# Weight halves behind the root, squares ahead of copies, and a root spread from four row groups to four banks

## The reference

```python
def rmsnorm(x, g):
    xf = x.astype(jnp.float32)
    y = xf * lax.rsqrt(jnp.mean(xf * xf, axis=-1, keepdims=True) + NORM_EPS)
    return (y * g.astype(jnp.float32)).astype(x.dtype)

    # in hybrid_layer
    x = x + rmsnorm(mixed @ w_out, norm_mix_post)
    h = rmsnorm(x, norm_ffn_pre)
    ...
    x = x + rmsnorm((jax.nn.gelu(ua) * ub) @ w_down, norm_ffn_post)
    x = x + rmsnorm(gate * e, norm_ple)
```

## Time and profile before

| | us |
|---|---|
| median of 3 runs | 4541.85 |
| lowest, highest | 4536.22, 4552.05 |
| profiled execution, first to last instruction | 4542.0 |
| TensorE busy in it | 4202.5 (93%) |
| VectorE busy | 1966.0 (43%) |
| ScalarE busy | 1514.9 (33%) |

### The profile page before, as it was taken

How to read it: one execution, slowest core, us unless ns; L and a number is a source line. 1 busy time by engine, 2 the same in 40 slices (tenths; PEclk the granted TensorE clock), 3 DMA queues, 4 the chain that set the end, 5 groups by cost and what they waited for, 6 DMA issues and landing times.

```text
span 4542.0 us, 73530 instructions
## 1 busy us (share of the span) xinstructions
PE 4202.5 (93%) x32028; PEld 3257.7 (72%) x32028; DVE 1966.0 (43%) x2957; ACT 1514.9 (33%) x2699; POOL 570.2 (13%) x402
## 2 busy tenths in 40 slices
PE   8899779899998999779899998988899999999999
PEld 6676776677776676776677776755688888667877
DVE  4536434455335536434455334357332231443332
ACT  3533233333333533233333333247221121343221
POOL 1215100011002215100011001012000000150000
PEclk9999899899998999999899998999999999999999
DMA  4122002244322132003244321100111111101222
GB/s 159 38 102 70 31 4 93 70 173 172 142 84 104 38 107 70 31 4 107 79 172 167 136 85 41 52 28 1 38 53 64 65 61 61 56 6 61 93 90 92
DMA packets 97681, 351.69 MB, mean 77 GB/s; under 512 B 10064, under 2 KB 13648, under 8 KB 95952
## 3 DMA queue, kind: packets, MB, share of 16 engines
q1 hardware_dynamic: 86480, 313.02, 20.0%
q10 hardware_dynamic: 10880, 33.96, 2.0%
HBM read 332.26 MB, written 14.68 MB: 76 GB/s over the span
## 4 chain that ended last, share of the span: by engine, by line
PE 82%; DVE 7%; ACT 3%; issue 3%; POOL 3%; ACTq 0%; DMA 0%; DVEq 0%; POOLq 0%; SPq 0%
PE ps L350 20%; PE ps L351 19%; PE ps L353 19%; PE ps L1344 7%; PE ps L2370 1%; PE ps L1889 1%; PE ps L391 1%; DVE sml L2445 1%; POOL e L2901 1%; ACT whi L297 1%; PE ps L2814 1%; POOL dd L1194 1%; PE ps L864 1%; POOL ops L1210 1%; POOL ops L1202 1%
## 5 line engine op out<-in xcount | busy, mean ns | idle before, releaser
L307 DVE TENSOR_TENSOR wlo<-ring,whi 128x1024 fp32r<-128x1024 f32 x494 | 623.7, 1263 | 1876.0 <-ACT whi L297 1875.6
L297 ACT CAST whi<-ring 128x1024 fp32r<-128x1024 f32 x494 | 517.4, 1048 | 2139.3 <-PE ps L353 1875.3
L350 PE MATMUL ps<-h_hi,whi 128*128 128x512 f32 x1424 | 597.1, 419 | 16.3 <-DVE h_lo L443 8.9
L351 PE MATMUL ps<-h_lo,whi 128*128 128x512 f32 x1424 | 569.2, 400 | 0.0
L353 PE MATMUL ps<-h_hi,wlo 128*128 128x512 f32 x1424 | 567.9, 399 | 0.0
L350 PE MATMUL ps<-hm_hi,whi 128*128 128x512 f32 (+1 forms) x1408 | 514.4, 365 | 16.5 <-DVE hm_lo L446 15.1
L351 PE MATMUL ps<-hm_lo,whi 128*128 128x512 f32 (+1 forms) x1408 | 480.3, 356 | 0.0
L353 PE MATMUL ps<-hm_hi,wlo 128*128 128x512 f32 (+1 forms) x1408 | 418.5, 355 | 0.0
L350 PEld LDWEIGHTS ps<-h_hi,whi 128*128 128x128 f32 x1424 | 272.9, 192 | 158.7 <-issue 62.4
L350 PE MATMUL ps<-ac_hi,whi 128*128 128x512 f32 x880 | 329.7, 375 | 3.0 <-DVE wlo L307 3.0
L350 PEld LDWEIGHTS ps<-hm_hi,whi 128*128 128x128 f32 x1408 | 267.1, 190 | 86.9 <-DVE hm_lo L446 20.4
(11 more groups left out here) (385 smaller groups left out, 7255.6 us busy)
## 6 DMA issues: line engine op xcount, KB each, us to landing
ring<-in_w SPq DMA_DIRECT2D x590, 512.0 KB, 3.3
h_spill<-h ACTq DMA_DIRECT2D x2, 2048.0 KB, 6.7
x_spill<-x ACTq DMA_DIRECT2D x2, 2048.0 KB, 14.6
m_spill<-m ACTq DMA_DIRECT2D x2, 2048.0 KB, 10.0
h_again<-h_spill ACTq DMA_DIRECT2D x2, 2048.0 KB, 8.9
ma<-m_spill ACTq DMA_DIRECT2D x2, 2048.0 KB, 10.1
x<-x_spill ACTq DMA_DIRECT2D x2, 2048.0 KB, 9.9
x<-in_x SPq DMA_DIRECT2D x4, 512.0 KB, 7.8
```

Of the source, the lines that this page charges most:

```text
L297: self.A.copy(self.hi[k % 2][:], raw).then_inc(self.s_cut_hi.h, 1)
L307: self.V.tensor_tensor(self.lo[k % 2][:], raw, self.hi[k % 2][:].bitcast(F32), ALU.subtract).then_inc(self.s_cut_lo.h, 1)
L350: T.matmul(ps[:, b, 0:cw], hi, xh(q, c0, cw), start=q == 0, stop=False, skip_group_check=True)
L351: T.matmul(ps[:, b, 0:cw], hi, xl(q, c0, cw), start=False, stop=False, skip_group_check=True)
```

## The change

Three edits to the norms.

1. **Cuts behind the root.** The dense products that end in a norm get `hold` = the last column's piece + 1, so that the piece after that is no longer cut ahead of the last column's work. `add_normed` and `norm_to` take `cut`: ScalarE makes that cut right behind `stat_root`, VectorE right behind `stat_inverse` and ahead of its wait for the spread. It is used at 9 norms: Z, ZF and E in both hybrid layers, and the three `mod_norm`s behind an `add_gated`. `first_cuts` of the first norm becomes `cut=1`, which is the same.
2. **Square, then copy.** For Z and ZF each column is squared from PSUM first and copied after.
3. **Four row groups to four banks.** Where four banks are given, `stat_spread` issues one matmul per quarter of the tokens whose operands are 32 partitions high (rows 32g to 32g+31 of the picking matrix and of `inv`), each into its own bank, and VectorE reads the spread as 4 pieces of 128 from four banks (`spread_of`, with the tile viewed alike by `by_bank`). It is used at 8 norms: the hybrid layers' first norms, Z, the norm behind Z, and E, in both layers. ZF keeps one bank and the `mod_norm`s two, with the old spread.

The lines added and taken away (unchanged lines left out):

```diff
@@ -396,6 +396,14 @@
+        if len(banks) == 4:
+            for g in range(4):
+                one = CONST["ident"] + 32 * g
+                rows = slice(32 * g, 32 * g + 32)
+                m = T.matmul(self.ps[:, banks[g], 0:w], self.con[rows, one:one + 1].to_broadcast([32, P]),
+                             self.inv[rows, 0:w], start=True, stop=True, skip_group_check=True)
+            m.then_inc(self.s_rsq.h, 1)
+            return
@@ -405,8 +413,18 @@
+    def spread_of(self, banks, si, cw):
+        if len(banks) == 4:
+            return self.ps[:, banks[0]:banks[0] + 4, 0:P]
+        return self.ps[:, banks[si], 0:cw]
+    def by_bank(self, banks, t):
+        return t.rearrange("p (g c) -> p g c", c=P) if len(banks) == 4 else t
-                first_cuts=False):
+                cut=None):
@@ -425,8 +443,8 @@
-            if first_cuts:
-                self.act_cuts(1)
+            if cut is not None:
+                self.act_cuts(cut)
@@ -449,13 +467,14 @@
-            if first_cuts:
-                self.dve_cuts(1)
+            if cut is not None:
+                self.dve_cuts(cut)
-                    i = V.scalar_tensor_tensor(dst[:, j, c0:c0 + cw], self.X[:, j, c0:c0 + cw], gain(j, si),
-                                               ps[:, banks[si], 0:cw], ALU.mult, ALU.mult)
+                    i = V.scalar_tensor_tensor(self.by_bank(banks, dst[:, j, c0:c0 + cw]),
+                                               self.by_bank(banks, self.X[:, j, c0:c0 + cw]), gain(j, si),
+                                               self.spread_of(banks, si, cw), ALU.mult, ALU.mult)
@@ -464,10 +483,10 @@
-    def add_normed(self, Z, gain, st, sums, pe_first=None, pe_last=None, act_last=None, dve_pair=None):
-        V, G, ps = self.V, self.G, self.ps
+    def add_normed(self, Z, gain, st, sums, banks, pe_first=None, pe_last=None, act_last=None, dve_pair=None, cut=None):
+        V, G = self.V, self.G
@@ -475,23 +494,28 @@
-            self.stat_spread(st, [st.bank])
+            self.stat_spread(st, banks)
+            if cut is not None:
+                self.act_cuts(cut)
+            if cut is not None:
+                self.dve_cuts(cut)
-                    V.scalar_tensor_tensor(Z[:, i, :], Z[:, i, :], gain(i), ps[:, st.bank, :], ALU.mult,
+                    z = self.by_bank(banks, Z[:, i, :])
+                    V.scalar_tensor_tensor(z, z, gain(i), self.spread_of(banks, 0, S), ALU.mult,
@@ -638,8 +662,8 @@
-        b_lo = self.norm_to(h, SEG1, lambda j, si: self.p1(gain, j), [6], st, h_hi, h_lo, ready=ready,
-                            first_cuts=layer == 0)
+        b_lo = self.norm_to(h, SEG1, lambda j, si: self.p1(gain, j), (4, 5, 6, 7), st, h_hi, h_lo, ready=ready,
+                            cut=1 if layer == 0 else None)
@@ -1851,24 +1875,24 @@
+            self.stat_square(st, n, ps[:, 2 + n % 4, :])
-            self.stat_square(st, n, ps[:, 2 + n % 4, :])
-                       pe_tick=pe_z, act_tick=act_z))
-        return self.first_norms(Z, b_z, st)
-    def first_norms(self, Z, b_z, st):
+                       pe_tick=pe_z, act_tick=act_z, hold=cols_z[-1][-1].cut + 1))
+        return self.first_norms(Z, b_z, st, self.ahead(cols_z[-1][-1].cut))
+    def first_norms(self, Z, b_z, st, cut):
-        b_add = self.add_normed(Z, lambda j: self.p1("post", j), st, [DT - 1])
+        b_add = self.add_normed(Z, lambda j: self.p1("post", j), st, [DT - 1], (2, 3, 4, 5), cut=cut)
-        return self.norm_to(self.view("h", 6144, DT, S), SEG1, lambda j, si: self.p1("fpre", j), [6],
+        return self.norm_to(self.view("h", 6144, DT, S), SEG1, lambda j, si: self.p1("fpre", j), (4, 5, 6, 7),
@@ -2037,8 +2061,8 @@
+            self.stat_square(st, n, ps[:, n % 4, :])
-            self.stat_square(st, n, ps[:, n % 4, :])
@@ -2047,7 +2071,7 @@
-                       down_act_tick, down_dve_tick))
+                       down_act_tick, down_dve_tick, hold=cols[-1][-1].cut + 1))
@@ -2114,7 +2138,7 @@
-        self.add_normed(ZF, lambda j: self.p1("fpost", j), st_z, [DT - 1], pe_first, pe_last, act_last, dve_pair)
+        self.add_normed(ZF, lambda j: self.p1("fpost", j), st_z, [DT - 1], [st_z.bank], pe_first, pe_last, act_last, dve_pair, e_piece + 1)
@@ -2145,12 +2169,13 @@
-                       dve_tick))
+                       dve_tick, hold=cols[-1][-1].cut + 1))
-        return self.add_normed(E, lambda j: self.p1("ple", j), st, [DT - 2, DT - 1])
+        return self.add_normed(E, lambda j: self.p1("ple", j), st, [DT - 2, DT - 1], (0, 1, 2, 3),
+                               cut=self.ahead(cols[-1][-1].cut))
@@ -2523,7 +2548,10 @@
-        go(*self.dense(cols, xh, xl, segs, banks_of, free, ready, pe_tick=pe_tick, act_tick=act_tick, dve_tick=dve_tick))
+        last = cols[-1][-1].cut
+        self.next_cut = self.ahead(last)
+        go(*self.dense(cols, xh, xl, segs, banks_of, free, ready, pe_tick=pe_tick, act_tick=act_tick, dve_tick=dve_tick,
+                       hold=last + 1 if st else None))
@@ -2880,7 +2908,7 @@
-        b_lo = self.mod_norm(0, 1, SEG2, st, squares=[DT - 1], sums=[DT - 2, DT - 1])
+        b_lo = self.mod_norm(0, 1, SEG2, st, squares=[DT - 1], sums=[DT - 2, DT - 1], cut=self.next_cut)
@@ -2888,7 +2916,7 @@
-        b_lo = self.mod_norm(1, 0, SEG2, st, squares=[DT - 1], sums=[DT - 2, DT - 1])
+        b_lo = self.mod_norm(1, 0, SEG2, st, squares=[DT - 1], sums=[DT - 2, DT - 1], cut=self.next_cut)
@@ -2905,7 +2933,7 @@
-        b_lo = self.mod_norm(1, 1, SEG1, st, squares=[DT - 1], sums=[DT - 2, DT - 1])
+        b_lo = self.mod_norm(1, 1, SEG1, st, squares=[DT - 1], sums=[DT - 2, DT - 1], cut=self.next_cut)
```

## The result

The changed kernel takes 4511.5 us in the median of 4 runs (4507.6 to 4518.9) against 4542.8 of the kernel before (4 runs, 4536.2 to 4552.1), a ratio of 0.9938, 95% interval 0.9924 to 0.9953: between 21 and 35 us less. Its profiled execution has a span of 4517.4 us (4518.9 as a run, the longest of the four), 24.6 less than the 4542.0 of before.

What follows compares the result with a forecast made beforehand. The prediction took TensorE's dense products to bound the kernel, with gains only where TensorE idles at norms. Terms 3.84 + 4.82 + 4.14 + 2.86 + 6.66 = 22.3 off 4542.0 gave 4520 us, range 4509 to 4533.

Steps and rivals of the forecast that it cites:

- the mod_norms: Three mod_norms: with both cuts out of line, the last column's addition starts at once, 2.22 us each, 6.66 in all.
- what bounds it: Whole kernel: TensorE's dense products bind it (82% of the chain); the edit only shortens the places where TensorE idles.
- Z, the norm behind it, ZF: Both hybrid layers: Z 2.41 us less, the norm behind it 1.28, ZF 1.43, each per layer.
- The order square, copy, root, cast: Sign at Z in the profile after: this order, with the root some 1.1 us after the last matmul.
- the spread: Four row groups overlap: 0.80 us for 2.08 at half clock, 1.28 less at each of three norms.
- row groups don't run side by side: Rival on the new spread: it keeps its 2.08 us, total gain 14.3, time 4528; chance 0.12.
- the new wait: Z and E: VectorE's half of the cut, not the spread, ends last, 2.0 us from reciprocal's start to first scaling.
- four pieces are free: Scalings reading four banks cost nothing extra; the rival, up to 0.63 us per call and 4560, had chance 0.04.
- E, layer 0: E's norm: the cut ahead of the sigmoid of the last column goes, 0.95 us, bounds 0.9 to 1.04.
- the clock takes some back: Rival at product restarts: half clock lasts longer or shorter; 8 us taken back gives 4528; chance 0.17.
- Every norm leaves TensorE at half clock: Premise of the clock rival: the product after each norm starts at half clock, 6.4 us behind one, 3.0 behind another.

Runs made afterwards that it cites:

- e4: The changed kernel run again with nothing edited, in a later comparison with the kernel before: ratio 0.9945 (0.9932 to 0.9957).
- e5: The changed kernel with the spread's matmuls back at full height (128 rows), still four banks and four pieces: 4517.2 us, ratio 0.9948 to the kernel before.
- e7: The changed kernel with VectorE's half of the cut at Z and E moved behind the last addition: 4513.7 us, ratio 0.9936 to the kernel before.
- e6: The kernel before with the cuts behind the root at the three mod_norms alone: ratio 0.9989 (0.9980 to 0.9998), 5.0 us less.
- e3: The kernel before with the square ahead of the copy at Z and ZF alone: ratio 0.9993 (0.9984 to 1.0002).
- e2: The kernel before with the weights' cuts behind the root alone, at 9 norms: ratio 0.9959 (0.9946 to 0.9971).

## Why the prediction was right

The forecast was 4520, range 4509 to 4533; the time is 4511.5 (4513.5 in e4), faster as forecast and near the range's low end. That it came so low is partly luck: the gate products' 2.8 and most of what the mod_norms gave beyond their 6.7 came by the clock, for which the sum had no term.

- *Right: what bounds it.* The halts were serial; what was taken out of them came off the end. Sum forecast 22.3, measured 23.9.
- *Right: Z, the norm behind it, ZF.* 3.69 forecast, 3.73 and 3.57 measured; root 1.49 earlier for 1.43. The order square, copy, root, cast is as forecast.
- *Right: the spread.* 0.80 forecast at half clock, 0.81 measured, eight overlapping records. The rival "row groups don't run side by side" falls: with the same four banks, only e5, which has no row groups, shows 2.08. The Trainium skill, "TensorE: Matmul & The Clock Gate", closing table of goals, has 3.07 times for four matmuls of 512 columns; with 128 columns the trace gives less: 2.08 / 0.81 = 2.6 times at half clock and 1.16 / 0.50 = 2.3 at full.
- *Right: the new wait.* From the reciprocal's start to the first scaling 1.98 at Z and 2.00 at E for 2.0, ended by VectorE's own half; e7 took it away and got 1.4 us.
- *Right: four pieces are free.* 736 for 737; the rival that would have made the kernel slower needed 350 ns more per call.
- *Mis-sized: the mod_norms.* Each was put at 2.22, at most 2.3: "with nothing ahead of it the addition starts at 3285.24". It starts at once, as said, and yet they are 2.38, 2.60 and 3.41, all above the bound. The cuts in line were worth 2.27. At the other two the way to the root shortened by 2.60 and 2.49, since the sum that took 0.87 and 0.65 (the earlier trace rows has the latter) now runs at full clock in 0.53 and 0.43; and the last spread took 1.16 for 2.08, another 0.92. I counted every norm's tail at the clock that it had before. The last spread is at half clock in all four profiles with this norm untouched, and at full clock in seven of the eight with it shortened. It isn't only that the spread comes earlier (3.4 behind the last matmul for 5.9): the clock also falls later, 5.4 to 5.8 behind the last matmul in those seven, where it fell 3.0 to 3.1 behind it in the untouched four. With the fall where it was, the spread would still have been at half clock. Why the fall moved is not shown. e6, which changes the mod_norms alone, has it too. The exception is e5, with the same code at this norm, where the clock fell 3.1 behind the last matmul:

```profile
4134.67 2.08 PE L412 MATMUL ps<-inv,con 128*128 128x128 f32 x8 [1.47 <-DVE inv L384]
```
- *Mis-sized: E, layer 0.* 0.95 forecast ahead of the root, 0.77 measured: the sum stood at full clock before and stands at half clock after, 0.2 the other way. In layer 1 it is 1.00. This is the clock's scatter: the root stands 4.73 and 4.96 behind the last matmul in the two profiles of the kernel before, and 3.96 and 3.74 in the two of the changed one.
- *Left out: the clock in the dense products.* Of the restarts, one loses 1.0 and one gains 0.5 in every profile of the shortened norms but e5's, and the rest scatters: the rival "the clock takes some back" came to little, 2.2 in the first pair of profiles. "Every norm leaves TensorE at half clock" was wrong for ZF, whose product restarts at full clock in both kernels. In the gate products 2.8 was gained. For them I had no term at all, and that part of the gain is seen, not explained.
- The rest, 25 us by the profiles and by e4 against 28 (21 to 35) by the first comparison, is within what either measures.

## What to carry to other kernels

In a serial chain behind a dense product, look for instructions that the next product needs but the chain doesn't, here the cuts of the weights. Put each behind the step that lets another engine go on, so that it runs beside that engine's work; then look which engine is late next, as it was VectorE's own half here. Don't price the chain's later steps at the clock that they had: with the head shorter, the same spread ran in 1.16 for 2.08 in five of six profiles. And don't read a clock loss or gain behind one halt from one profile: the same kernel had 3.0 and 6.1 us of half clock at the same place.

## What was not expected of the hardware

- TensorE's clock stays up for the first microseconds of a halt, but not for a fixed time: in the twelve profiles it fell 2.2 to 5.9 us behind the last matmul, while TensorE still had short sums and spreads. Full-height spreads at Z that start 2.7 us behind the last matmul (e5) or 3.7 (e3) run at full clock, 1.16; at 3.2 (e2) 1.32 and 1.16; at 4.2 the kernel before has 1.93, 1.76, 1.84 and 1.16 in its two profiles. The exception of e5 was at half clock 3.4 behind it.
- A product that restarts earlier isn't always at full clock earlier by as much: at one norm 1.0 of 2.6 us went back, in five profiles of six.
- Four row groups over 192 columns took 0.61 at full and 1.02 at half clock, where the full-height spread took 3.14 at half: 3.1 times, against 2.6 over 128 columns. The full-height one also has ten records for the same columns, the new one eight.
